# Expert layer on one core: the gates of the first dense tile placed by 128 indirect transfers with addition

## The chip, the core and the metric

One NeuronCore of one Trainium2 chip runs one program. Its engines work side by side and meet only at semaphores: TensorE (PE in the profile, with its weight loads as PEld), VectorE (DVE), ScalarE (ACT), GpSimd (POOL) and the sync engine (SP), which issues most of the DMA transfers. The metric is the device time of one execution in microseconds. Three runs of the kernel before took 1687.2, 1688.26 and 1694.93 us, median 1688.26.

## The reference

One layer of a decoder on 512 tokens of width 1024, all in f32. A conditioning vector gives shift, scale and gate for two sub-layers. Sub-layer 1 mixes tokens (a gated unit and an attention with forgetting). Sub-layer 2, around which this change lies, retrieves single-neuron experts: each token has 8 heads, each head picks 16 of 16384 experts by products of two sub-keys, so that a token has 128 picks. Cut to what matters:

```
q = (xt @ w_query).reshape(t, 8, 2, 128)
scores = einsum('thpd,hpnd->thpn', q, sub_keys)
sv, si = top_k(scores, 16)                       # 16 rows i and 16 columns j of a 128 x 128 grid
cand   = sums of the 16 x 16 pairs;  top_s, pos = top_k(cand, 16)
idx    = i * 128 + j at pos;         gate = softmax(top_s)      # 8 heads x 16 picks per token
out[t] = sum over picks e of  gate[t,e] * gelu(expert_u[idx[t,e]] . x[t]) * expert_v[idx[t,e]]
```

Two heads of a token may pick the same expert, one head never picks one twice. After it come the gated residual and a final RMSNorm.

## The kernel before

The 512 tokens are four tiles of 128. Tile 0 is the sparse one: for each of its 128 picks GpSimd gathers 128 rows of `expert_u` (4 KB each, one per token) by an indirect transfer, and VectorE takes the dot product with the token (`dot`, L1497); later the same is done with `expert_v` (`add`, L1503). The gathered rows go through a ring of 8 places, four in `shared` and four in `hT`.

Tiles 1 to 3 are the dense ones. Their activations are computed for all 16384 experts: `products` (L1097 to L1099) multiplies a block m of 128 experts with the 384 tokens, 24 matmuls of 384 columns, for m = 0 to 127. ScalarE rounds the block (`round_u`, L764), VectorE takes the rest of the rounding (`rest_of_u`, L1490, always one block ahead) and ScalarE reads the result through gelu (L772) and SP stores it. Afterwards `outputs` (L1152 to L1156) multiplies gate times gelu with `expert_v`, again for all experts. For this the gates must stand in a dense array: `g_dram` (`gates_dense`), 24 groups of 16 tokens, each of 128 x (128 x 16) numbers, 1 MB, with the expert's j as row, then i and token.

The dense gates of a tile are built by one-hot products. When its picks and gates are known (`gates`, L1464, signal `gates_ready`), PE transposes i, j and gate (`turn`, L921) and ScalarE copies them (L814). Then for each half group of 8 tokens VectorE writes two one-hot arrays by comparison with a ramp (`hot_rows`, L1477), ScalarE scales one of them by the gates (`gate_rows`, L784), PE multiplies them per token (`build`, L1112: 8 matmuls) and ScalarE copies the two banks (`copy_built`, L793). Per 16 tokens SP stores a group.

The order of all this is written out by hand, alike on each engine. In the loop over n = 1, 2, 3 the selection of tile n runs on VectorE in 11 segments, between which `BESIDE[n]` products stand (3 in all for n = 1, 18 for n = 2 and for n = 3); then `gates(n)`, one product (`BEFORE_TURN`), the turn, two products (`AFTER_TURN`), and 16 steps of one half group's build and one product each. These last are called the chunks of the tile here. In the chunks VectorE takes 4 and 3 dots in turn per group of 16 tokens, so 28 per tile. So n = 1 holds products 0 to 21, n = 2 holds 22 to 58, n = 3 holds 59 to 95. The products 96 to 111 stand in a loop with two dots each (`LOOP_AT` = 12, counted in bodies of 8), and the last 16 with 12 dots.

GpSimd issues the gathers in program order (`gather_rows`, L589 and L601): rows 0 to 3 as soon as tile 0's picks are known, rows 4 to 7 after the turn of the first dense tile, each later row when the dot that used its place is done. A dot waits for the gather of its row; VectorE works in program order, so whatever stands behind the dot waits too, and `rest_of_u` stands there, for which the next product on PE waits.

Of the kernel before, what the change touches and what calls it, by code (L numbers as in the profile page):

```python
# [67 lines left out]
LOOP_AT = 12  # L68
DOTS_BESIDE = (4, 3)
DOTS_IN_CHUNKS = DENSE * CHUNKS // 2 * sum(DOTS_BESIDE)  # L70
# [34 lines left out]
def plan_banks():  # L105
# [28 lines left out]
    jobs += [(("turn", d), 5) for d in range(DENSE)]  # L134
# [7 lines left out]
def program(nc, x, cT, w_ada, b_ada, norm1_g, w_in, b_f, sg_ln_g, sg_ln_b, sg_wT, sg_bT,  # L142
# [5 lines left out]
    with ExitStack() as ctx:  # L148
# [107 lines left out]
        g_dram = nc.dram_tensor("gates_dense", (GROUPS, P, NKEYS * GROUP), F32).ap()  # L256
        a_dram = nc.dram_tensor("gelu_dense", (NKEYS // A_STEPS, P, A_STEPS * DTOK), F32).ap()
# [14 lines left out]
        turned = ada[:, 2 * D:2 * D + 6 * P].rearrange("p (b c t) -> p b c t", b=2, c=3)  # L272
        iota128 = ada[:, 2 * D + 6 * P:2 * D + 7 * P]
# [59 lines left out]
        gates_ready, iota_made = sem("gates_ready"), sem("iota_made")  # L333
        hot_made, hot_gated, built = sem("hot_made"), sem("hot_gated"), sem("built")
# [49 lines left out]
        def _(sp):  # L384
# [53 lines left out]
            sp.dma_start(keysT, sub_keysT).then_inc(keys_in, 16)  # L438

# [17 lines left out]
            for n in range(1, NT):  # L457
# [69 lines left out]
        def _(pool):  # L527
# [11 lines left out]
            link(nc.gpsimd.memset(gate[:, :], 1.0))  # L539
            link(nc.gpsimd.memset(tri, 1.0))  # L540
# [42 lines left out]
            def gather_rows(table, which, used):  # L583

                def one_round(i, half, first):
# [17 lines left out]

                one_round(0, 0, True)
                one_round(0, 1, False)
# [10 lines left out]
        def _(act):  # L617
# [161 lines left out]
            def gate_rows(half):  # L779
                act.wait_ge(hot_made, half + 1)  # L780
                for q in range(HTOK):
                    token = half % (P // HTOK) * HTOK + q
                    rows = hot_i[:, half % HALVES, q, :]
                    ins = nc.scalar.activation(rows, rows, ACT.Copy, scale=turned[:, half * HTOK // P % 2, 2, token:token + 1])  # L784
# [15 lines left out]
            for n in range(1, NT):  # L800
# [860 lines left out]
```

## Time and profile before

| | us |
|---|---|
| median of the runs | 1688.26 |
| the profiled execution | 1689.51 |
| its span, first to last instruction | 1687.8 |
| PE busy | 1587.2 (94%) |
| DVE busy | 1258.3 (75%) |
| ACT busy | 664.9 (39%) |
| POOL busy | 391.9 (23%) |
| mean granted TensorE clock | 0.98 |

The profile is of one execution. All durations are read from it, and the profiled execution's own time is 1.7 us above its span. Up to some 490 us the first sub-layer and the queries run, from some 495 to 1132 us the 128 products with the three builds beside them, then the outputs. A busy PE is not a PE at its peak, since matmuls overlap; the pace of a stage is read from the distance of equal instructions instead.

### The profile page before, as it was taken

The numbers are of one execution on the slowest core, as the hardware profiler recorded it, in microseconds if no ns is written. First come the engines' busy times: TensorE is split into PE (matmuls) and PEld (weight loads), VectorE is DVE, ScalarE is ACT, GpSimd is POOL, SyncE is SP. The second block draws the span as 40 slices with busy tenths as digits, with TensorE's granted clock in tenths as the row PEclk, the third lists the DMA queues.
The fourth block names the chain that finished last, engine by engine and source line by source line (L and its number), as shares of the span: only waits on it lengthen the run. The fifth ranks groups of instructions, "written<-read, shape, count | busy, mean of one in ns | idle before, by whom it ended". The sixth has DMA issues, their size and how long they took to land.

```text
span 1687.8 us, 22615 instructions
## 1 busy us (share of the span) xinstructions
PE 1587.2 (94%) x7605; PEld 1292.7 (77%) x7605; DVE 1258.3 (75%) x2268; ACT 664.9 (39%) x1227; POOL 391.9 (23%) x326
## 2 busy tenths in 40 slices
PE   1899988999999999999989999799999999999995
PEld 0454465554559999999989999798888888888884
DVE  6448364439957987899788988558888878788887
ACT  2111132221337852588336853233333333333333
POOL 1101400000002320033001346413344334334420
PEclk9989989999999999999999999999999999999998
DMA  9765420000127994489736999987999999999982
GB/s 361 275 229 181 149 76 0 1 0 1 50 85 278 363 360 150 160 325 357 278 135 224 361 387 413 402 314 261 367 352 345 354 357 354 329 362 359 344 315 87
DMA packets 172770, 426.26 MB, mean 253 GB/s; under 512 B 13068, under 2 KB 62220, under 8 KB 169496
## 3 DMA queue, kind: packets, MB, share of 16 engines
q1 hardware_dynamic: 86400, 265.89, 42.2%
q0 software_dynamic: 36864, 134.23, 21.8%
q10 hardware_dynamic: 49432, 25.19, 5.3%
q8 instruction: 41, 0.67, 0.2%
q14 instruction: 33, 0.27, 0.0%
HBM read 372.84 MB, written 52.43 MB: 252 GB/s over the span
## 4 chain that ended last, share of the span: by engine, by line
PE 87%; DVE 6%; DMA 3%; ACT 2%; issue 1%; ACTq 1%; SPq 0%; DVEq 0%
PE bank L1152 10%; PE bank L1153 10%; PE bank L1156 10%; PE bank L1097 10%; PE bank L1099 10%; PE bank L1098 10%; PE bank L1043 7%; PE bank L951 5%; PE bank L1112 5%; PE bank L1026 3%; PE bank L961 3%; PE bank L921 1%; DMA weights<-in_w_ada 1%; PE bank L1053 1%; ACTq L842 1%
## 5 line engine op out<-in xcount | busy, mean ns | idle before, releaser
L1097 PE MATMUL bank<-h_hi,u_hi 128*128 128x384 f32 x1024 | 350.7, 343 | 22.0 <-DVE u_lo L1490 13.2
L1098 PE MATMUL bank<-h_lo,u_hi 128*128 128x384 f32 x1024 | 345.0, 337 | 0.0
L1099 PE MATMUL bank<-h_hi,u_lo 128*128 128x384 f32 x1024 | 345.0, 337 | 0.0
L1152 PE MATMUL bank<-v_hi,w_hi 128*128 128x512 f32 x768 | 299.2, 390 | 1.7 <-DVE w_lo L1597 1.6
L1153 PE MATMUL bank<-v_lo,w_hi 128*128 128x512 f32 x768 | 298.8, 389 | 0.0
L865 ACT ACTIVATE v_hi<-weights 128x1024 fp32r<-128x1024 f32 x128 | 135.8, 1061 | 330.2 <-PE bank L1156 264.3
L1156 PE MATMUL bank<-v_hi,w_lo 128*128 128x512 f32 x768 | 236.4, 389 | 0.0
L1593 DVE TENSOR_TENSOR v_lo<-weights,v_hi 128x1024 fp32r<-128x1024 f32 x128 | 157.7, 1232 | 95.2 <-ACT v_hi L865 93.0
L1490 DVE TENSOR_TENSOR u_lo<-weights,u_hi 128x1024 fp32r<-128x1024 f32 x128 | 155.9, 1223 | 95.8 <-PE bank L1099 72.7
L1097 PEld LDWEIGHTS bank<-h_hi,u_hi 128*128 128x128 f32 x1024 | 194.7, 190 | 25.3 <-DVE u_lo L1490 12.8
L1098 PEld LDWEIGHTS bank<-h_lo,u_hi 128*128 128x128 f32 x1024 | 194.8, 190 | 0.0
L1099 PEld LDWEIGHTS bank<-h_hi,u_lo 128*128 128x128 f32 x1024 | 194.3, 190 | 0.0
L1152 PEld LDWEIGHTS bank<-v_hi,w_hi 128*128 128x128 f32 x768 | 144.1, 188 | 33.4 <-DVE v_lo L1593 2.4
L1156 PEld LDWEIGHTS bank<-v_hi,w_lo 128*128 128x128 f32 x768 | 144.2, 188 | 30.0
L1153 PEld LDWEIGHTS bank<-v_lo,w_hi 128*128 128x128 f32 x768 | 144.2, 188 | 29.7
L601 POOL DMA_INDIRECT hT<-in_expert_u,idx_slot x64 | 78.6, 1228 | 290.1 <-DVE hT L1497 200.7
L601 POOL DMA_INDIRECT hT<-in_expert_v,idx_slot x64 | 102.8, 1606 | 172.6 <-DVE y L1503 157.3
L1477 DVE TENSOR_TENSOR weights<-ada 128x1024 f32<-128x1024 f32 x96 | 113.5, 1224 | 35.8 <-PE bank L1112 24.2
L764 ACT ACTIVATE u_hi<-weights 128x1024 fp32r<-128x1024 f32 x128 | 135.1, 1057 | 0.8 <-DMA weights<-in_uT 0.8
L784 ACT ACTIVATE weights<-weights,ada 128x128 f32<-128x128 f32 x384 | 117.7, 389 | 38.5 <-DVE weights L1477 38.5
L601 POOL DMA_INDIRECT shared<-in_expert_v,idx_slot x64 | 90.4, 1412 | 179.1 <-DVE y L1503 149.3
L601 POOL DMA_INDIRECT shared<-in_expert_u,idx_slot x64 | 72.6, 1134 | 204.4 <-DVE shared L1497 187.3
(233 smaller groups left out, 2179.6 us busy)
## 6 DMA issues: line engine op xcount, KB each, us to landing
weights<-in_uT SPq DMA_DIRECT2D x128, 512.0 KB
weights<-in_expert_v SPq DMA_DIRECT2D x128, 512.0 KB, 7.8
weights<-in_w_ada SPq DMA_DIRECT2D x12, 2048.0 KB, 10.3
gates_dense<-weights SPq DMA_DIRECT2D x24, 1024.0 KB
weights<-gates_dense ACTq DMA_DIRECT2D x16, 1536.0 KB
shared<-gelu_dense SPq DMA_DIRECT2D x64, 384.0 KB, 8.9
gelu_dense<-weights SPq DMA_DIRECT2D x32, 384.0 KB
gelu_dense<-ada SPq DMA_DIRECT2D x32, 384.0 KB
```

The lines of the kernel that those rows point to most:

```text
L601: nc.gpsimd.indirect_dma_start(ring(r % ROWS), None, table, bass.IndirectOffsetOnAxis(idx_slot[:, half, r:r + 1], 0))\
L764: nc.scalar.activation(u_hi[:, r % RAW, :], u_raw[:, r % RAW, :], ACT.Copy).then_inc(u_hi_made, 1)
L865: nc.scalar.activation(v_hi[:, r % 2, :], v_raw[:, r % RAW, :], ACT.Copy).then_inc(v_hi_made, 1)
L1043: ins = nc.tensor.matmul(b[:, :], h2T(t)[:, k, :], w[:, k, :], start=(k == 0), stop=(k == KC - 1))
L1097: nc.tensor.matmul(a, uh[:, k, :], h2_hi[:, :, k, :], start=(k == 0), stop=False)
L1098: nc.tensor.matmul(a, uh[:, k, :], h2_lo[:, :, k, :], start=False, stop=False)
L1099: ins = nc.tensor.matmul(a, ul[:, k, :], h2_hi[:, :, k, :], start=False, stop=(k == KC - 1))
L1152: nc.tensor.matmul(acc, wh, v_hi[:, r % 2, cols], start=begin, stop=False)
L1153: nc.tensor.matmul(acc, wh, v_lo[:, r % RAW, cols], start=False, stop=False)
L1156: ins = nc.tensor.matmul(acc, wl, v_hi[:, r % 2, cols], start=False, stop=end)
L1490: tt(u_lo[:, r % LOW, :], u_raw[:, r % RAW, :], u_hi[:, r % RAW, :].bitcast(F32), ALU.subtract).then_inc(u_lo_made, 1)
L1593: tt(v_lo[:, r % RAW, :], v_raw[:, r % RAW, :], v_hi[:, r % 2, :].bitcast(F32), ALU.subtract).then_inc(v_lo_made, 1)
```

## The change

The first dense tile (`d` = 0, n = 1) is no longer built by one-hot products. Its part of `g_dram`, 8 groups, is filled with zeros by 8 transfers of SP from `gate_sparse`, which GpSimd has set to zero at the start; they stand behind the load of the sub-keys, and `gates(0)` waits for them before it writes `gate_sparse`. `gates(1)` writes the normalised gates and, in two more small instructions, the address of each pick in `g_dram` (`sent_gate`, `sent_place`); a constant per token (`token_place`) is made in five small instructions on VectorE beforehand. GpSimd then issues 128 indirect transfers, one for each pick (head h, place k): each sends 128 single f32 numbers, one per token, from SBUF to `g_dram`, and adds them to what stands there. The 16 transfers of a head follow one another freely, since their addresses are all different; ahead of the first of the next head GpSimd waits until all before have landed, since two heads of a token may have the same address. In GpSimd's order they stand between the first round of gathers (rows 0 to 7) and the second (rows 8 to 15).

The transposes, the one-hot arrays, the scaling, the build matmuls, the copies and the stores of this tile go, and with them the 16 steps of its chunks: n = 1 holds products 0 to 5, n = 2 holds 6 to 42, n = 3 holds 43 to 79, and the loop takes products 80 to 111 (`LOOP_AT` = 10). The 28 dots that stood in the first tile's chunks move: dots 0 to 27 now stand in the chunks of n = 2, 28 to 55 in those of n = 3, and 64 instead of 32 in the loop. ScalarE waits for all transfers ahead of its first load of gates. The rest is index arithmetic. Its core:

```diff
+SCATTERED = 1
+BUILT = DENSE - SCATTERED
+LOOP_AT = 10
 DOTS_BESIDE = (4, 3)
-DOTS_IN_CHUNKS = DENSE * CHUNKS // 2 * sum(DOTS_BESIDE)
+DOTS_IN_CHUNKS = BUILT * CHUNKS // 2 * sum(DOTS_BESIDE)
...
+        g_places = g_dram.rearrange("g p n -> (g p n)").rearrange("(n a) -> n a", a=1)
...
+        sent_gate, sent_place = [[turned[:, d % 2, c] for d in range(SCATTERED)] for c in range(2)]
+        sent_place = [p.bitcast(U32) for p in sent_place]
+        token_place = misc[:, 96:97]
+        token_low, token_u = misc[:, 97:98], misc[:, 98:99].bitcast(U32)
...
+            sp.wait_ge(zeros_made, 1)
+            for g in range(SCATTERED * CHUNKS):
+                sp.dma_start(g_dram[g].rearrange("p (a n) -> p a n", n=NSEL),
+                             gate_sparse[:, :].unsqueeze(1).broadcast_to([P, NKEYS * GROUP // NSEL, NSEL])).then_inc(g_zeroed, 16)
...
-                for c in range(CHUNKS):
+                for c in range(CHUNKS if n > SCATTERED else 0):
                     for h in range(HALVES):
                         product(m, m % BODY)
                         m += 1
-                    g = (n - 1) * CHUNKS + c
+                    g = (n - 1 - SCATTERED) * CHUNKS + c
                     sp.wait_ge(build_read, (g + 1) * GROUP // BATCH)
-                    sp.dma_start(g_dram[g], staging[g % 2].rearrange("p i t -> p (i t)")).then_inc(g_stored[g % 2], 16)
+                    sp.dma_start(g_dram[SCATTERED * CHUNKS + g], staging[g % 2].rearrange("p i t -> p (i t)")).then_inc(g_stored[g % 2], 16)
...
+            nc.gpsimd.memset(gate_sparse[:, :], 0.0).then_inc(zeros_made, 1)
+            nc.gpsimd.iota(token_u, [[1, 1]], base=0, channel_multiplier=1).then_inc(token_made, 1)
...
                             if r == ROWS // 2 and not which:
-                                wait_full(pool, "turn", 0)
+                                pool.wait_ge(places_ready, 1)
...
+                def scatter(d, h):
+
+
+                    if h == 0:
+                        pool.wait_ge(places_ready, d + 1)
+                    if d == 0 and h == 0:
+                        pool.wait_ge(g_zeroed, 16 * SCATTERED * CHUNKS)
+                    else:
+                        pool.wait_ge(scattered, 16 * TOPK * (d * PH + h))
+                    for k in range(h * TOPK, (h + 1) * TOPK):
+                        nc.gpsimd.indirect_dma_start(g_places, bass.IndirectOffsetOnAxis(sent_place[d][:, k:k + 1], 0),
+                                                     sent_gate[d][:, k:k + 1], None, compute_op=ALU.add).then_inc(scattered, 16)
+
                 one_round(0, 0, True)
+                for d in range(0 if which else SCATTERED):
+                    for h in range(PH):
+                        scatter(d, h)
                 one_round(0, 1, False)
...
-                for _ in range(BEFORE_TURN):
+                for _ in range(BEFORE_TURN if d >= SCATTERED else BEFORE_TURN + AFTER_TURN):
                     product(m)
                     m += 1
+                if d < SCATTERED:
+                    continue
+                e = d - SCATTERED
                 b = wait_full(act, "turn", d)
-                if d >= 2:
-                    act.wait_ge(hot_gated, (d - 1) * P // HTOK)
+                if d >= 2 and d - 2 < SCATTERED:
+                    act.wait_ge(scattered, 16 * NSEL * (d - 1))
+                elif d >= 2:
+                    act.wait_ge(hot_gated, (e - 1) * P // HTOK)
                 release(nc.scalar.activation(turned[:, d % 2], b[:, 0:3 * P].rearrange("p (c t) -> p c t", c=3), ACT.Copy), "turn", d)
                 product(m)
                 m += 1
-                gate_rows(d * P // HTOK)
+                gate_rows(e * P // HTOK)
                 product(m)
                 m += 1
-                gate_rows(d * P // HTOK + 1)
-                for h in range(HALVES * d * CHUNKS, HALVES * (d + 1) * CHUNKS):
+                gate_rows(e * P // HTOK + 1)
...
-                act.wait_ge(g_stored[b], 16 * GROUPS // 2)
-            act.wait_ge(built, DTOK // BATCH)
+                act.wait_ge(g_stored[b], 16 * BUILT * CHUNKS // 2)
+            act.wait_ge(scattered, 16 * NSEL * SCATTERED)
+            act.wait_ge(built, BUILT * P // BATCH)
...
+                if d < SCATTERED:
+                    for _ in range(AFTER_TURN):
+                        product(m)
+                        m += 1
+                    continue
+                e = d - SCATTERED
+                pe.wait_ge(gates_ready, e + 1)
                 transposes(("turn", d), [picks(n)[2], picks(n)[3], gate[:, :]])
...
-                if n >= 2:
+                if n - 2 >= SCATTERED:
...
-                into = (gate if n else gate_sparse)[:, :].rearrange("p (h k) -> p h k", h=PH)
+                if n == 0:
+                    dve.wait_ge(g_zeroed, 16 * SCATTERED * CHUNKS)
+                into = gate_sparse[:, :] if n == 0 else sent_gate[n - 1] if n <= SCATTERED else gate[:, :]
+                into = into.rearrange("p (h k) -> p h k", h=PH)
                 ins = tt(into, gh, gate_sum.unsqueeze(2).broadcast_to([P, PH, TOPK]), ALU.mult)
-                if n:
+                if n > SCATTERED:
                     ins.then_inc(gates_ready, 1)
                 else:
                     link(ins)
+                if 0 < n <= SCATTERED:
+
+                    sel_i, sel_j = picks(n)[2:4]
+                    link(stt(out=sel_j, in0=sel_j, scalar=float(NKEYS), in1=sel_i, op0=ALU.mult, op1=ALU.add))
+                    ts(sent_place[n - 1], sel_j, float(GROUP), token_place, ALU.mult, ALU.add).then_inc(places_ready, 1)
+                    if n > 1:
+                        dve.wait_ge(places_ready, n)
...
+            dve.wait_ge(token_made, 1)
+            link(nc.vector.tensor_copy(token_place, token_u))
+            link(ts(token_u, token_u, GROUP - 1, None, ALU.bitwise_and))
+            link(nc.vector.tensor_copy(token_low, token_u))
+            link(tt(token_place, token_place, token_low, ALU.subtract))
+            link(stt(out=token_place, in0=token_place, scalar=float(P * NKEYS), in1=token_low, op0=ALU.mult, op1=ALU.add))
```

On GpSimd (POOL), at the first round of gathers, this stands in a row before (L601 are the gathers, `bank5_full` is the turn of the first dense tile):

```order
L601 DMA shared<-in_expert_u,idx_slot 128x1024 [waits idx_staged]
L601 DMA shared<-in_expert_u,idx_slot 128x1024 x3
L601 DMA hT<-in_expert_u,idx_slot 128x1024 [waits bank5_full]
L601 DMA hT<-in_expert_u,idx_slot 128x1024 x3
L589 COPY idx_slot<-idx 128x8
L601 DMA shared<-in_expert_u,idx_slot 128x1024 [waits idx_staged,dot_done]
L601 DMA shared<-in_expert_u,idx_slot 128x1024 [waits dot_done] x3
```

And now (L617 are the gathers, L631 the transfers with addition), first the beginning of the piece and then its end:

```order
L617 DMA shared<-in_expert_u,idx_slot 128x1024 [waits idx_staged]
L617 DMA shared<-in_expert_u,idx_slot 128x1024 x3
L617 DMA hT<-in_expert_u,idx_slot 128x1024 [waits places_ready]
L617 DMA hT<-in_expert_u,idx_slot 128x1024 x3
L631 DMA gates_dense<-ada 6291456x1 [waits g_zeroed,places_ready]
L631 DMA gates_dense<-ada 6291456x1 x15
L631 DMA gates_dense<-ada 6291456x1 [waits scattered]
L631 DMA gates_dense<-ada 6291456x1 x15
```

```order
L631 DMA gates_dense<-ada 6291456x1 x15
L631 DMA gates_dense<-ada 6291456x1 [waits scattered]
L631 DMA gates_dense<-ada 6291456x1 x15
L605 COPY idx_slot<-idx 128x8
L617 DMA shared<-in_expert_u,idx_slot 128x1024 [waits idx_staged,dot_done]
L617 DMA shared<-in_expert_u,idx_slot 128x1024 [waits dot_done] x3
```

Between the gather of row 7 and that of row 8 there are now 128 transfers and eight waits; nothing else of GpSimd's program has moved.

On VectorE, at the gates of the first dense tile (L1461 to L1464), before, with the first one-hot arrays (L1477) and dots (L1497) behind them:

```order
L1490 TENSOR_TENSOR u_lo<-weights,u_hi 128x1024 x4
L1461 TENSOR_REDUCE misc<-gate 128x8
L1462 RECIPROCAL misc<-misc 128x8
L1464 TENSOR_TENSOR gate<-gate,misc 128x128
L1490 TENSOR_TENSOR u_lo<-weights,u_hi 128x1024
L1477 TENSOR_TENSOR weights<-ada 128x1024 x2
L1490 TENSOR_TENSOR u_lo<-weights,u_hi 128x1024
L1477 TENSOR_TENSOR weights<-ada 128x1024 x2
L1490 TENSOR_TENSOR u_lo<-weights,u_hi 128x1024
L1477 TENSOR_TENSOR weights<-ada 128x1024 x2
L1490 TENSOR_TENSOR u_lo<-weights,u_hi 128x1024
L1497 SCALAR_TENSOR_TENSOR shared,act_w<-shared,y 128x1024 x2
```

And now, with the address's two instructions (L1520, L1521) and the selection of the next tile (L1410 and on) right behind:

```order
L1545 TENSOR_TENSOR u_lo<-weights,u_hi 128x1024 x4
L1506 TENSOR_REDUCE misc<-gate 128x8
L1507 RECIPROCAL misc<-misc 128x8
L1512 TENSOR_TENSOR ada<-gate,misc 128x128
L1520 SCALAR_TENSOR_TENSOR hT<-hT 128x128
L1521 TENSOR_SCALAR ada<-hT,misc 128x128
L1545 TENSOR_TENSOR u_lo<-weights,u_hi 128x1024 x3
L1410 MAX final_row<-shared 128x8 x8
L1413 MAX_INDEX final_row<-final_row,shared 128x8 x8
```

The 16 steps with one-hot arrays are gone from this place, and with them the first 28 dots.

On VectorE, in the chunks of the second dense tile, before; these dots are numbers 28 and on:

```order
L1477 TENSOR_TENSOR weights<-ada 128x1024 x2
L1490 TENSOR_TENSOR u_lo<-weights,u_hi 128x1024
L1477 TENSOR_TENSOR weights<-ada 128x1024 x2
L1490 TENSOR_TENSOR u_lo<-weights,u_hi 128x1024
L1497 SCALAR_TENSOR_TENSOR hT,act_w<-hT,y 128x1024 x2
L1477 TENSOR_TENSOR weights<-ada 128x1024 x2
L1490 TENSOR_TENSOR u_lo<-weights,u_hi 128x1024
L1497 SCALAR_TENSOR_TENSOR hT,act_w<-hT,y 128x1024 x2
L1477 TENSOR_TENSOR weights<-ada 128x1024 x2
```

And now at the same place, dots 0, 1, 2 and on (L1552):

```order
L1532 TENSOR_TENSOR weights<-ada 128x1024 x2
L1545 TENSOR_TENSOR u_lo<-weights,u_hi 128x1024
L1552 SCALAR_TENSOR_TENSOR shared,act_w<-shared,y 128x1024 x2
L1532 TENSOR_TENSOR weights<-ada 128x1024 x2
L1545 TENSOR_TENSOR u_lo<-weights,u_hi 128x1024
L1552 SCALAR_TENSOR_TENSOR shared,act_w<-shared,y 128x1024 x2
L1532 TENSOR_TENSOR weights<-ada 128x1024 x2
L1545 TENSOR_TENSOR u_lo<-weights,u_hi 128x1024
L1552 SCALAR_TENSOR_TENSOR hT,act_w<-hT,y 128x1024
L1532 TENSOR_TENSOR weights<-ada 128x1024 x2
L1545 TENSOR_TENSOR u_lo<-weights,u_hi 128x1024
L1552 SCALAR_TENSOR_TENSOR hT,act_w<-hT,y 128x1024 x2
```

The dots that stand in the second tile's chunks are now the first ones of all, and the ninth of them needs a row that GpSimd gathers only behind the 128 transfers.

## Rows read from the trace of the kernel before

**Rows 1.** The page: busy time by engine; the chain by engine and line.

```profile
PE 1587.2 (94%) x7605; PEld 1292.7 (77%) x7605; DVE 1258.3 (75%) x2268; ACT 664.9 (39%) x1227; POOL 391.9 (23%) x326
...
PE 87%; DVE 6%; DMA 3%; ACT 2%; issue 1%; ACTq 1%; SPq 0%; DVEq 0%
PE bank L1152 10%; PE bank L1153 10%; PE bank L1156 10%; PE bank L1097 10%; PE bank L1099 10%; PE bank L1098 10%; PE bank L1043 7%; PE bank L951 5%; PE bank L1112 5%; PE bank L1026 3%; PE bank L961 3%; PE bank L921 1%; DMA weights<-in_w_ada 1%; PE bank L1053 1%; ACTq L842 1%
```

**Rows 2.** ACT timeline, gelu reads (L772): start us, us, what, [idle before <-releaser].

```profile
511.01 0.49 ACT L772 ACTIVATE ada<-bank 128x384 f32<-128x384 f32 x1 [2.72 <-PE bank L1099]
...
619.19 0.49 ACT L772 ACTIVATE weights<-bank 128x384 f32<-128x384 f32 x1 [2.62 <-issue]
...
623.35 0.49 ACT L772 ACTIVATE ada<-bank 128x384 f32<-128x384 f32 x1 [2.72 <-PE bank L1099]
```

**Rows 3.** The chain in order of time, 490 to 720: start us, us, what.

```profile
524.00 1.78 PE bank L1112 x16
```

**Rows 4.** Busy us (instructions) by engine, then PEclk, DMA share, GB/s, by window.

```profile
525.42:614.62 89.20, 89.20 (x603) 89.20 (x602) 81.23 (x97) 70.83 (x173) 29.71 (x29) 1.00 0.97 355
623.35:706.51 83.16, 78.08 (x439) 76.97 (x438) 68.40 (x230) 29.21 (x40) 0.00 (x0) 0.98 0.51 172
1004.77:1050.45 45.68, 45.68 (x266) 45.68 (x265) 38.58 (x55) 15.87 (x22) 29.49 (x25) 1.00 1.03 414
```

**Rows 5.** DVE timeline around the gates of the first dense tile.

```profile
490.84 1.23 DVE L1484 TENSOR_TENSOR h_lo<-y,h_hi 128x1024 fp32r<-128x1024 f32 x1 [6.06 <-PE bank L1043]
...
508.61 0.29 DVE L1464 TENSOR_TENSOR gate<-gate,misc 128x128 f32<-128x128 f32 x1
```

**Rows 6.** POOL timeline: indirect transfers, each with its idle time before.

```profile
433.12 0.95 POOL L601 DMA_INDIRECT shared<-in_expert_u,idx_slot  x1 [0.30 <-issue]
434.37 0.95 POOL L601 DMA_INDIRECT shared<-in_expert_u,idx_slot  x1 [0.30 <-issue]
...
518.37 1.96 POOL L601 DMA_INDIRECT hT<-in_expert_u,idx_slot  x1 [0.30 <-issue]
520.64 1.97 POOL L601 DMA_INDIRECT hT<-in_expert_u,idx_slot  x1 [0.30 <-issue]
...
531.27 1.17 POOL L601 DMA_INDIRECT shared<-in_expert_u,idx_slot  x1 [7.21 <-DVE shared L1497]
532.75 1.07 POOL L601 DMA_INDIRECT shared<-in_expert_u,idx_slot  x1 [0.30 <-issue]
...
557.80 1.05 POOL L601 DMA_INDIRECT shared<-in_expert_u,idx_slot  x1 [0.89 <-POOL idx_slot L589]
```

**Rows 7.** DVE timeline, first and ninth dot in the second dense tile's chunks.

```profile
719.88 1.22 DVE L1497 SCALAR_TENSOR_TENSOR hT<-hT,y 128x1024 f32<-128x1024 f32 x1
...
744.81 1.22 DVE L1497 SCALAR_TENSOR_TENSOR hT<-hT,y 128x1024 f32<-128x1024 f32 x1
```

**Rows 8.** DMA queues and issues: KB each, us to landing.

```profile
q0 software_dynamic: 36864, 134.23, 21.8%
...
out<-xs SPq DMA_DIRECT2D x4, 512.0 KB, 2.7
...
ada<-in_norm_g SPq DMA_DIRECT2D x1, 512.0 KB, 3.7
...
misc<-in_cT SPq DMA_DIRECT2D x1, 4.0 KB, 1.7
```

**Rows 9.** SP timeline after the last loads, and a window of the attention.

```profile
218.69 0.34 SPq L438 DMA_DIRECT2D ada<-in_sub_keysT  x1
...
255.00:375.00 120.00, 108.85 (x443) 62.68 (x442) 48.15 (x93) 32.63 (x64) 0.00 (x0) 1.00 0.00 1
```

**Rows 10.** The chain from 1060 to 1110, and ACT behind it.

```profile
1068.49 12.32 DMA weights<-in_uT
...
1081.89 14.01 ACTq L842
...
1103.09 0.49 ACT L772 ACTIVATE weights<-bank 128x384 f32<-128x384 f32 x1 [4.38 <-PE bank L1099]
```

More of the change, by code:

```diff
@@ L133, in plan_banks @@
         jobs += query_jobs(n, QUERY_PAIRS[0]) + query_jobs(n, QUERY_PAIRS[1])
-    jobs += [(("turn", d), 5) for d in range(DENSE)]
+    jobs += [(("turn", d), 5) for d in range(SCATTERED, DENSE)]
     place, count = {}, [0] * 8
@@ L333, in program @@
         gates_ready, iota_made = sem("gates_ready"), sem("iota_made")
+        zeros_made, g_zeroed, token_made = sem("zeros_made"), sem("g_zeroed"), sem("token_made")
+        places_ready, scattered = sem("places_ready"), sem("scattered")
         hot_made, hot_gated, built = sem("hot_made"), sem("hot_gated"), sem("built")
@@ L783, in gate_rows @@
                     rows = hot_i[:, half % HALVES, q, :]
-                    ins = nc.scalar.activation(rows, rows, ACT.Copy, scale=turned[:, half * HTOK // P % 2, 2, token:token + 1])
+                    ins = nc.scalar.activation(rows, rows, ACT.Copy,
+                                               scale=turned[:, (SCATTERED + half * HTOK // P) % 2, 2, token:token + 1])
                 ins.then_inc(hot_gated, 1)
@@ L816, in _ @@
                 m += 1
-                gate_rows(d * P // HTOK)
+                gate_rows(e * P // HTOK)
                 product(m)
                 m += 1
-                gate_rows(d * P // HTOK + 1)
-                for h in range(HALVES * d * CHUNKS, HALVES * (d + 1) * CHUNKS):
+                gate_rows(e * P // HTOK + 1)
+                for h in range(HALVES * e * CHUNKS, HALVES * (e + 1) * CHUNKS):
                     copy_built(2 * h)
@@ L826, in _ @@
                     m += 1
-                    if h + HALVES < HALVES * (d + 1) * CHUNKS:
+                    if h + HALVES < HALVES * (e + 1) * CHUNKS:
                         gate_rows(h + HALVES)
@@ L1129, in _ @@
                     m += 1
-                if d == 0:
+                if e == 0:
                     for t in range(NT):
@@ L1133, in _ @@
                             wait_read(pe, "h2T", t, s)
-                for h in range(HALVES * d * CHUNKS, HALVES * (d + 1) * CHUNKS):
+                for h in range(HALVES * e * CHUNKS, HALVES * (e + 1) * CHUNKS):
                     build(h)
@@ L1159, in _ @@
             wait_read(pe, "turn", DENSE - 1)
-            pe.wait_ge(build_read, DTOK // BATCH)
+            pe.wait_ge(build_read, BUILT * P // BATCH)
             for r in range(BODY):
@@ L1475, in hot_rows @@
                 for which, rows in ((1, hot_j), (0, hot_i)):
-                    key = turned[:, half * HTOK // P % 2, which, at:at + HTOK]
+                    key = turned[:, (SCATTERED + half * HTOK // P) % 2, which, at:at + HTOK]
                     ins = tt(rows[:, half % HALVES], iota128.unsqueeze(1).broadcast_to([P, HTOK, P]),
@@ L1526, in _ @@
                 gates(n)
-                for _ in range(BEFORE_TURN):
+                for _ in range(BEFORE_TURN if d >= SCATTERED else BEFORE_TURN + AFTER_TURN):
                     product(m)
                     m += 1
+                if d < SCATTERED:
+                    continue
+                e = d - SCATTERED
                 wait_read(dve, "turn", d)
                 for h in range(HALVES):
-                    hot_rows(d * P // HTOK + h)
+                    hot_rows(e * P // HTOK + h)
                     product(m)
                     m += 1
-                for h in range(HALVES * d * CHUNKS, HALVES * (d + 1) * CHUNKS):
-                    if h + HALVES < HALVES * (d + 1) * CHUNKS:
+                for h in range(HALVES * e * CHUNKS, HALVES * (e + 1) * CHUNKS):
+                    if h + HALVES < HALVES * (e + 1) * CHUNKS:
                         hot_rows(h + HALVES)
```

2 lines of the change are left out of this document (removed).

## The prediction

> **What bounds the kernel now.** I read the page first. PE is busy for 94% of the span and makes 87% of the chain that ended last, with the build matmuls (L1112) as 5% of it [rows 1]. A busy PE may still be paced by another engine, so the second view is ScalarE's timeline, cut down to the gelu that reads each product: its distances are the pace. Without builds it is 4.16 us (619.19 to 623.35), with them 5.95 (15 steps in the 89.20 us of the first window) [rows 2, 4]. The chain says why: in each chunk step the 16 records of one build take 1.78 us of the path [rows 3], and 4.16 + 1.78 is 5.94. PE sets the pace in both, with VectorE at 91% of the window beside it (81.23 of 89.20 us) [rows 4]. What the change takes off PE is therefore worth its full length there.
>
> The other thing to see is how VectorE, PE and GpSimd hang together. VectorE runs in program order, PE needs its `u_lo` for each product and gets it one product ahead. A dot stands between two of them and waits for a row that GpSimd gathered. In the kernel before GpSimd is far ahead: it has nothing at all to do from 623 to 706 us [rows 4]. The change fills just this time, and the question is whether it ends in time.
>
> **What goes.** From the gelu of product 2 (511.01) to that of product 22 (623.35) are 20 products in 112.34 us [rows 2]. At 4.16 each they take 83.2, so the turn and the 16 builds of the first dense tile cost 29.1 us beyond the products, 28.5 of them 16 times 1.78 [rows 3]. The 16 products themselves move to the loop, where 11 of them take 45.68 us with two dots each, 4.15 apiece [rows 4]. Gain: **-29.1 us**. The stores, copies and scalings of this tile lie beside PE's work and give nothing more.
>
> **What is hidden.** GpSimd's memset and ramp at the start stand before all work. The five small instructions for `token_place` stand ahead of the second selection, at whose end VectorE waits 6.06 us for PE [rows 5]; they are far shorter than that, so 0, and at most some 2 us without this cover. The zeros are 8 MB behind the sub-keys, issued at 218.69; in a window of 120 us behind them the DMA share is 0.00 [rows 9], and SP's next work comes at some 490 us. At a quarter of the 355 GB/s of [rows 4] 8.4 MB take 94 us and still end inside that window. 0.
>
> **The 128 transfers.** The places are ready two small instructions behind the gates at 508.61, so at 509.5 [rows 5]. First come the gathers of rows 4 to 7. From start to start one costs 1.25 us (433.12 to 434.37, VectorE in selection work), 1.48 (531.27 to 532.75, beside dots and `u_lo`) or 2.27 (518.37 to 520.64, where one-hot arrays are written) [rows 6]. Four at 1.48 end at 515.4.
>
> A scatter of single numbers with addition isn't in the trace. Each addresses 128 rows as a gather does, and GpSimd makes the descriptors for as many, so gathers are the nearest rows. Lower end 0.95, the duration of one without the 0.30 gap (here no other signal stands between two transfers); upper end 2.27. VectorE does selection work most of this time, with a `u_lo` every 4.16 us, so I take 1.30, near the first kind: 128 x 1.30 = 166.4. On top come seven waits between heads, each from the last issue to its landing. Small transfers land in 1.7 (4 KB in), 2.7 (a 512 KB store to HBM) or 3.7 us (a 512 KB load by row) [rows 8]; I take the store's 2.7, so 18.9. T = 185.3, from 133.5 (128 x 0.95 + 7 x 1.7) to 316.5 (128 x 2.27 + 7 x 3.7). GpSimd is through at 700.7.
>
> The page "DMA: Bandwidth & Descriptors" of the Trainium skill (Anatomy of one DMA) puts the fixed cost of such a transfer at about 2.0 us, nearly all of it the receipt of the write. By it the seven waits would be 14 and not 18.9 us, and the forecast 5 us lower; the landing times of 1.7 to 3.7 here agree with it.
>
> Behind the transfers GpSimd copies the next indices and waits for the copy (0.89 us ahead of the start at 557.80 [rows 6], 1.0 with the copy), issues the gather of row 8 (1.3) and it lands (3.7): 706.7.
>
> **When row 8 is wanted.** The first eight dots have their rows. The ninth stands 24.9 us behind the first of its tile's chunks (719.88, 744.81) [rows 7]. That is 121.5 us behind the gelu at 623.35, with which the segments of n = 2 begin. In the changed kernel that gelu comes 29.1 + 16 x 4.16 = 95.7 us earlier, so the ninth dot is due at 649.1. VectorE is one product ahead, which covers 4.2 us. The stall is S = 706.7 - 649.1 - 4.2 = **+53.4 us**. Behind GpSimd's transfers wait the gathers of rows 8 to 15, behind the dot on VectorE wait the one-hot arrays and `u_lo`, behind these PE. Nothing gives it back later: the stages behind are at PE's pace. In general S = T - 132.
>
> Two small terms. After the stop near 1090 us the next gelu waits 4.38 us where 2.72 is usual [rows 2, 10], so +1.6 for the restart. And the loop with two gathers per product gets 16 products longer. It moves 414 GB/s with a DMA share of 1.03 [rows 4], right at its limit; what a product asks for (three times 0.524 MB and 0.197 MB of stores) in 4.16 us is 425. Over 16 products the missing 11 GB/s are 0.7 MB, 1.8 us, which lengthens the wait that stands there already (12.32 us for `u`, 14.01 for ScalarE's issue of the gate load [rows 10]). I take +2, from 0 to 10 (the whole ring of 8 rows late, 4.2 MB at 414).
>
> **Sum.** -29.1 + 53.4 + 1.6 + 2.0 = +27.9. Against the profiled execution, 1689.5, that is 1717.4. The median of the runs lies 1.2 below that execution, so **1716 us**.
>
> **Rivals.** *The transfers are cheap.* GpSimd might need less for a single number than for a row, and without the gap. At the lower end T is 133.5 and S 1.6, the sum -24 and the time 1664; below T = 132 the gain is whole and the time 1661. For it speaks the missing signal between two transfers; against it that no start to start in the trace is below 1.25 us, which already gives T = 179. It decides at T = 157.5, 1.08 us per transfer, where the sum is zero.
>
> *In between.* 1.02 to 1.15 us per transfer leave the time within 0.5%: the stall eats the gain and no more.
>
> *GpSimd is disturbed.* A gather takes 1.96 us instead of 0.95 where VectorE writes one-hot arrays [rows 6], two inputs from SBUF at once. If the same happened beside all of the transfers, T is 316.5, S 184.5 and the time 1847. Against it: in this stretch VectorE mostly selects, and beside that the duration was 0.95.
>
> The page "SBUF - State Buffer" of the Trainium skill (Who interferes with whom) says that a `tensor_tensor` with both inputs in SBUF contends with GpSimd's reads only, and infers that making descriptors needs the write side. By this no transfer is disturbed, each costs 1.25 and the time is 1710. The 1.96 us of the row speak against it, so I don't go by it.
>
> *The DMA engines are the pace.* The gathers' queue took 21.8% of 16 engines' span for 36864 packets [rows 8], 0.16 us each, 9 per engine and transfer. If adding one number takes an engine as long as moving one such packet, a transfer takes 1.44 us, T is 203 and the time 1734. If it takes twice that, since the old value must be read first, T is 387, S 255 and the time 1918. A full round trip of 1.7 us for each number, one after the other, would be 15 us per transfer and nearly 2 ms; that end is there, but in the trace packets of one queue overlap.
>
> **How the numbers follow.** A change of 0.5%, 8.4 us, is about what can be told from none here. Forecast with its neighbours (1.15 to 1.75 us per transfer, GpSimd or DMA as the pace): 0.50. Cheap transfers: 0.18. In between: 0.12. Disturbed or paced at 1.75 us and more: 0.20. Faster therefore 0.18, same 0.12, slower 0.70. The range goes from the cheap end, 1663, to 1800, which is a T of 270; it leaves some 0.05 below and 0.13 above. The likeliest case alone has 1698 to 1775.
>
> **What would show it.** In the profile after: 128 transfers on GpSimd from some 515 to 700 us, their start to start near 1.3 and seven gaps of some 2.7; a stop of VectorE before its ninth dot, near 650 us, of some 55 us with the gather as what ended it; products at 4.16 us from product 0 on to product 26, without the step to 5.95 near 525; a third of the build line's records gone; the loop's pace still 4.16. If the last transfer is over before 650, the forecast is wrong and the gain stands. If the starts are right and the stop is absent, my reading of the dots' order is wrong. If the products before 625 us are slower than 4.16, the transfers disturb something that I have left out.

## The result and the profile after

The changed kernel takes 1806.6 us, median of 4 runs (1804.6 to 1807.7), where the kernel before takes 1689.5 beside it. The ratio is 1.069, with a 95% interval of 1.067 to 1.071: slower by 117 us. The span of the profiled execution went from 1687.8 to 1802.9, so +115.1.

The page of the changed kernel: busy time, the chain by engine and line, and the group of the 128 transfers (L631; busy, mean ns | idle before).

```profile
PE 1560.3 (87%) x7346; PEld 1266.4 (70%) x7346; DVE 1224.4 (68%) x2243; ACT 609.3 (34%) x1066; POOL 633.3 (35%) x456
...
q0 software_dynamic: 55296, 134.31, 22.9%
...
PE 73%; POOL 12%; DVE 5%; DMA 4%; issue 4%; ACT 2%; ACTq 1%; SPq 0%; DVEq 0%; POOLq 0%
POOL gates_dense L631 11%; PE bank L1197 9%; PE bank L1198 9%; PE bank L1201 9%; PE bank L1136 7%; PE bank L1137 7%; PE bank L1138 7%; PE bank L1082 6%; PE bank L990 5%; PE bank L1065 3%; PE bank L1000 3%; PE bank L1151 2%; DMA gates_dense<-ada 1%; PE bank L960 1%; DMA weights<-in_w_ada 1%
...
L631 POOL DMA_INDIRECT gates_dense<-ada x128 | 217.3, 1698 | 55.5 <-issue 41.6
```

GpSimd now stands on the chain with 12%, where it did not stand at all [rows 1]. A transfer takes it 1698 ns on average, and the queue of its transfers has 55296 packets instead of 36864 [rows 8], 144 more for each of the 128.

GpSimd's timeline where the transfers begin, where VectorE has stopped, and at their end (columns as in [rows 6]):

```profile
514.94 0.94 POOL L617 DMA_INDIRECT hT<-in_expert_u,idx_slot  x1 [0.30 <-issue]
516.18 2.05 POOL L631 DMA_INDIRECT gates_dense<-ada  x1 [0.31 <-issue]
...
547.18 1.56 POOL L631 DMA_INDIRECT gates_dense<-ada  x1 [0.30 <-issue]
551.25 1.56 POOL L631 DMA_INDIRECT gates_dense<-ada  x1 [2.50 <-DMA gates_dense<-ada]
...
559.65 3.21 POOL L631 DMA_INDIRECT gates_dense<-ada  x1 [0.30 <-issue]
...
663.99 1.56 POOL L631 DMA_INDIRECT gates_dense<-ada  x1 [0.30 <-issue]
665.86 1.56 POOL L631 DMA_INDIRECT gates_dense<-ada  x1 [0.30 <-issue]
...
787.17 1.56 POOL L631 DMA_INDIRECT gates_dense<-ada  x1 [0.30 <-issue]
...
789.83 1.02 POOL L617 DMA_INDIRECT shared<-in_expert_u,idx_slot  x1 [0.90 <-POOL idx_slot L605]
```

The transfers run from 516.2 to 788.7 us, so T, the prediction's name for the length of this block, is 272.6. At rest one takes 1.56 us and the next starts 0.30 later (663.99 to 665.86). Beside VectorE's work, up to 653 us, 16 of the first 60 take 2.0 to 3.2 us (559.65). Between two heads GpSimd idles 2.50 us and less (551.25).

VectorE around its ninth dot (L1552), and ScalarE's reads of the products around it, the first of them to be held beside [rows 2]:

```profile
648.67 1.22 DVE L1552 SCALAR_TENSOR_TENSOR hT<-hT,y 128x1024 f32<-128x1024 f32 x1
...
794.42 1.23 DVE L1552 SCALAR_TENSOR_TENSOR shared<-shared,y 128x1024 f32<-128x1024 f32 x1 [144.53 <-DMA shared<-in_expert_u,idx_slot]
```

```profile
511.29 0.49 ACT L804 ACTIVATE ada<-bank 128x384 f32<-128x384 f32 x1 [2.72 <-PE bank L1138]
...
527.93 0.49 ACT L804 ACTIVATE ada<-bank 128x384 f32<-128x384 f32 x1 [2.72 <-PE bank L1138]
...
650.80 0.48 ACT L804 ACTIVATE ada<-bank 128x384 f32<-128x384 f32 x1
...
800.79 0.47 ACT L804 ACTIVATE weights<-bank 128x384 f32<-128x384 f32 x1
...
806.50 0.47 ACT L804 ACTIVATE weights<-bank 128x384 f32<-128x384 f32 x1
```

The ninth dot, free to go at 649.9, waits 144.53 us for the gather of row 8, and ScalarE sees the next product at 800.79 instead of some 6 us behind 650.80. From 511.29 to 527.93 four products came at 4.16 each: the step to 5.95 that stood there in the kernel before is gone.

The windows of the stop and of the loop (columns as in [rows 4]):

```profile
660.00:785.00 125.00, 0.00 (x0) 0.00 (x0) 0.00 (x0) 0.00 (x0) 97.19 (x63) 0.51 0.20 0
1057.00:1182.00 125.00, 125.00 (x723) 125.00 (x722) 104.84 (x149) 43.27 (x60) 82.92 (x67) 1.00 1.03 413
```

In 125 us nothing works but GpSimd. The DMA engines are busy for 0.20 of it at 0 GB/s, TensorE's granted clock is 0.51, its lower level of 1.2 GHz. Behind the stop TensorE's first product starts at that level. Below are the window of its first 9 records and, for comparison, one from the kernel of the third experiment behind its own shorter stop, with 18:

```profile
799.12:801.85 2.73, 2.73 (x9) 2.73 (x9) 2.73 (x5) 2.73 (x9) 2.43 (x2) 0.50 0.86 297
```

```profile
723.27:728.88 5.61, 5.61 (x18) 5.61 (x19) 5.61 (x8) 4.64 (x13) 4.40 (x4) 0.50 0.96 322
```

Here the next gelu, at 806.50, still comes after 5.71 us, no later than usual with a build, so in this kernel the lower clock costs nothing that shows. In the three kernels below that keep a stop (half of the transfers, without addition, half of the rows) 17 or 18 records ran at the lower level and the same interval is 6.84, 6.87 and 6.77 us instead of 5.89: there it costs about 1 us. The loop runs at its old pace with a DMA share of 1.03, over twice the length.

The balance of the spans: -29.1 for the builds, +144.0 for the stop (149.99 from one gelu to the next instead of 6.01) and +1.5 in the wait ahead of the last products, which is 17.9 us instead of 16.4. That is +116.4 against +115.1 measured.

### The profile page after: what moved, and what is told of

Same layout as the page of the kernel before. It is cut to its first block, busy times and chain, and to the rows that moved or that the text cites. A ratio compares the mean times of both kernels' runs of the same rounds, so it can differ in the third digit from the quotient of the medians.

```text
span 1802.9 us, 22177 instructions
## 1 busy us (share of the span) xinstructions
PE 1560.3 (87%) x7346; PEld 1266.4 (70%) x7346; DVE 1224.4 (68%) x2243; ACT 609.3 (34%) x1066; POOL 633.3 (35%) x456
## 3 DMA queue, kind: packets, MB, share of 16 engines
q0 software_dynamic: 55296, 134.31, 22.9%
## 4 chain that ended last, share of the span: by engine, by line
PE 73%; POOL 12%; DVE 5%; DMA 4%; issue 4%; ACT 2%; ACTq 1%; SPq 0%; DVEq 0%; POOLq 0%
POOL gates_dense L631 11%; PE bank L1197 9%; PE bank L1198 9%; PE bank L1201 9%; PE bank L1136 7%; PE bank L1137 7%; PE bank L1138 7%; PE bank L1082 6%; PE bank L990 5%; PE bank L1065 3%; PE bank L1000 3%; PE bank L1151 2%; DMA gates_dense<-ada 1%; PE bank L960 1%; DMA weights<-in_w_ada 1%
## 5 line engine op out<-in xcount | busy, mean ns | idle before, releaser
L631 POOL DMA_INDIRECT gates_dense<-ada x128 | 217.3, 1698 | 55.5 <-issue 41.6
L1552 DVE SCALAR_TENSOR_TENSOR shared<-shared,y 128x1024 f32<-128x1024 f32 x64 | 76.5, 1220 | 146.4 <-DMA shared<-in_expert_u,idx_slot 146.3
L617 POOL DMA_INDIRECT hT<-in_expert_v,idx_slot x64 | 113.2, 1769 | 171.0 <-DVE y L1558 141.0
L617 POOL DMA_INDIRECT hT<-in_expert_u,idx_slot x64 | 83.6, 1306 | 241.4 <-DVE hT L1552 156.7
L617 POOL DMA_INDIRECT shared<-in_expert_v,idx_slot x64 | 94.7, 1480 | 178.9 <-DVE y L1558 164.3
L816 ACT ACTIVATE weights<-weights,ada 128x128 f32<-128x128 f32 x256 | 78.5, 389 | 170.1 <-DVE weights L1532 170.1
```

The costliest lines, as they stand in the source:

```text
L617: nc.gpsimd.indirect_dma_start(ring(r % ROWS), None, table, bass.IndirectOffsetOnAxis(idx_slot[:, half, r:r + 1], 0))\
L631: nc.gpsimd.indirect_dma_start(g_places, bass.IndirectOffsetOnAxis(sent_place[d][:, k:k + 1], 0), sent_gate[d][:, k:k + 1], None, compute_ ...
```

## The experiments

The first four ran on one chip, where the kernel before took 1687.6 us.

**No transfer.** In `gather_rows` and at ScalarE's last wait (its wait for the transfers ahead of a later turn goes as well):

```diff
-                    for h in range(PH):
-                        scatter(d, h)
+                    pass
...
-            act.wait_ge(scattered, 16 * NSEL * SCATTERED)
```

> Leaves out all 128 transfers (the gates of the first dense tile stay zero); zeros, addresses and the order of everything else stay. Theory A (the loss is the row that stands behind the transfers on GpSimd, and nothing else): VectorE's wait of 144.5 us before the ninth dot is gone, the products come every 4.16 us up to product 21, and the time is 1806.6 - 144.5 + 0 to 4 for what was covered, so 1662 to 1666; that is the -29 us of the builds and +2 for the longer loop against 1689.5. Rival B (a part of the loss is in the zeros, the addresses or the longer loop): above 1672.

1661.1 us (1659.7 to 1662.8), ratio 0.983 (0.980 to 0.986). A second time, on another chip, 1660.4 and 0.985 (0.983 to 0.987). Theory A holds, and the time is even a little below its 1662 to 1666. Of the 29.1 us that the builds are worth 26.5 and 26.7 arrive, so zeros, addresses and the longer loop cost together some 2.5 us, and the whole loss comes with the transfers. The difference of the profiled spans is 1802.9 - 1661.0 = 141.9 (144.7 against the second one's 1658.2), and the products alone differ by 144, against a wait of 144.5.

**Half of the transfers** (ScalarE's waits count half as many).

```diff
-                    for h in range(PH):
+                    for h in range(PH // 2):
```

> Leaves out the last four of the eight heads, so 64 transfers remain. Theory A: they end where the first 64 of the changed kernel end, at 660.4 us, row 8 lands some 5.7 us later, at 666, and the ninth dot, due at 649.9, waits some 16 us; PE loses some 12 of them and the time is about 1674 to 1680. A stall in proportion to the number of transfers (half of 144.5) would give 1734, so the point T = 132 from which the transfers cost anything is tested too. Rival B (disturbance by additions all over the stage): half of the loss, about 1734.

```profile
L631 POOL DMA_INDIRECT gates_dense<-ada x64: 1559/1564/2590, 516.1 to 656.6; - x64
```

```profile
DVE shared L1552 <- DMA shared<-in_expert_u,idx_slot: 12.6, 1, 12.6
```

(A source view: duration in ns min/median/max, first and last start. A waits view: us in total, times, longest.) 1679.4 us, ratio 0.994 (0.991 to 0.996). Half of the transfers do not cost half of 144.5: VectorE waits 12.6 us. The loss has a threshold. Before the ninth dot is due some 130 us of transfers are free, behind it each costs its full length. T minus VectorE's wait is 129.5 here (656.6 + 1.6 - 516.1 = 142.1), and 128.1 with all of them.

**Transfers without addition.**

```diff
-                                                     sent_gate[d][:, k:k + 1], None, compute_op=ALU.add).then_inc(scattered, 16)
+                                                     sent_gate[d][:, k:k + 1], None).then_inc(scattered, 16)
```

> The 128 transfers write their numbers without adding (where two heads of a token pick the same expert the later one stays, so the sum of such pairs is left out). Tells what makes one transfer 1.56 us on GpSimd where a gather of a row takes 0.94. If it is the addition (the old value has to be described too), one falls to about 0.95, T to about 128 x 1.25 + 128 x 0.25 of disturbance + 14 = 206 and the time to about 1740. If it is the single number or the direction into HBM, 1.56 stays and the time is 1800 to 1810.

```profile
L631 POOL DMA_INDIRECT gates_dense<-ada x128: 963/967/1982, 515.9 to 711.9; - x128
```

```profile
DVE shared L1552 <- DMA shared<-in_expert_u,idx_slot: 69.0, 1, 69.0
```

```profile
q0 software_dynamic: 40960, 134.31, 21.0%
```

1730.7 us, ratio 1.024 (1.021 to 1.027). The transfer falls from 1563 to 967 ns, as long as a gather at rest [rows 6], T falls to 711.9 + 1.0 - 515.9 = 197 and the wait to 69.0. So it is the addition that costs GpSimd 0.60 us, not the single number and not the direction; what GpSimd does in that time is not shown. The packets change too: 40960 - 36864 are 32 per plain transfer, and with addition it is 144. But they are not what GpSimd's time follows: a gather also has 144 (36864 for 256 of them [rows 8]) and takes 0.95 [rows 6].

**Half of the rows in each transfer.** On another chip, one run:

```diff
-bass.IndirectOffsetOnAxis(sent_place[d][:, k:k + 1], 0), sent_gate[d][:, k:k + 1], ...
+bass.IndirectOffsetOnAxis(sent_place[d][0:P // 2, k:k + 1], 0), sent_gate[d][0:P // 2, k:k + 1], ...
```

> Each of the 128 transfers sends only the numbers of tokens 0 to 63 (the other half of the first dense tile's gates is left out). Tells whether a transfer costs GpSimd by its rows or by itself. By rows: 0.78 us instead of 1.56, T about 173 and the time about 1705. By itself: 1.56 and 1806. A plain transfer took 0.97 and one with addition 1.56; if these are a fixed part and one per row with two descriptors against three, it lies between, near 0.9, T near 190 and the time near 1720.

```profile
L631 POOL DMA_INDIRECT gates_dense<-ada x128: 1405/1410/3510, 517.0 to 767.1; - x128
```

```profile
q0 software_dynamic: 47104, 134.28, 22.0%
```

1789.6 us, with T at 251.5 and VectorE's wait at 125.0. My middle guess is wrong: 64 rows take 1410 ns and 128 take 1563, by these two points an estimated 2.4 ns per row and 1.26 us for the transfer itself. Smaller transfers hardly help GpSimd; whether fewer and fuller ones would wasn't run. A transfer has 80 packets now ((47104 - 36864) / 128), so with addition it is one per number and 16 more.

**The transfers spread over GpSimd's program.** The addition stays, the whole layer is computed. Gates and addresses get a stretch of `ada` of their own, so that the third tile's turn needn't wait for the transfers, and behind the gather of each row some transfers follow (the first rounds of gathers are written out for it instead of looped):

```diff
-        sent_gate, sent_place = [[turned[:, d % 2, c] for d in range(SCATTERED)] for c in range(2)]
+        sent_gate, sent_place = [ada[:, 2 * D + 7 * P:3 * D]], [ada[:, 3 * D:3 * D + P]]
...
+def sent_after(row):
+    # transfers behind the gather of a row: 128 in all
+    return {7: 48, 35: 35}.get(row, 1 if row > 7 and row % 5 else 0)
...
+                        if not which and isinstance(i, int):
+                            for _ in range(sent_after((2 * i + half) * STAGED + r)):
+                                next(transfers)
```

> All 128 transfers, but spread over GpSimd's program: 48 (three heads) behind the gather of row 7, 35 behind that of row 35, the others one at a time behind the gathers of rows 8 to 63, in four of five. The gates and places lie in a stretch of their own, so that no turn waits for the transfers. Theory A: 48 transfers end near 624 us, before row 8's place is free, no dot waits long, and the time is that of the kernel without transfers, 1662 to 1668, 1.4% under the kernel before. Rival B (it is the work of the transfers, wherever they stand): GpSimd's and the DMA's extra work slows the chunks, and the time is above 1680.

1675.9 us, ratio 0.993 (0.990 to 0.996). The stop is gone and the kernel is faster than before, but 15 us above the kernel without transfers, between the two theories. Up to product 80 its products keep, but for fractions, that kernel's distances; then 82, 84 and 86 take 8.4, 8.8 and 6.9 us. VectorE waits there for gathers (waits from 905 to 950 us):

```profile
DVE shared L1562 <- DMA shared<-in_expert_u,idx_slot: 9.7, 5, 4.2
...
DVE hT L1562 <- DMA hT<-in_expert_u,idx_slot: 6.1, 3, 4.2
```

**Another division:** `{7: 54, 35: 44}`, 10 beside rows 8 to 27, 20 beside rows 36 to 55.

> As e4_spread with another division: 54 transfers behind row 7, 10 beside rows 8 to 27, 44 behind row 35, 20 beside rows 36 to 55. e4_spread lost its 12 us where the loop begins (products 82 to 86 at up to 8.8 us), with transfers until 923 us. Theory A (GpSimd runs late there because its transfers stand in the last chunks, where it has no time left beside the gathers; the transfers cost nothing where GpSimd would wait anyway): this stop is gone, the time is 1661 to 1666, the same as without any transfer, and 1.3 to 1.6% under the kernel before. Rival B (the transfers cost the stage something wherever they stand, some 0.1 us each): it stays near 1675.

1672.4 us, ratio 0.990 (0.988 to 0.992), between the two theories. The products keep the pace of the kernel without transfers up to 76, and again lose it where the last transfers stand in the chunks (waits from 895 to 925 us):

```profile
DVE hT L1562 <- DMA hT<-in_expert_u,idx_slot: 10.9, 4, 5.6
```

**A third division:** `{7: 54, 35: 46}`, one behind each of rows 8 to 27 and 36 to 43.

> As e5_spread2 with the 128 transfers divided 54 behind row 7, one behind each of rows 8 to 27, 46 behind row 35, one behind each of rows 36 to 43. In e5_spread2 the products kept the pace of the kernel without transfers up to product 76 and lost 1 us at 77 to 79, 5 us at 81 and 2.5 us in the loop, where the DMA share is 1.03 and a late ring is not made up. Theory A (what costs is a ring of gathered rows that is not full when the loop begins; transfers that end well before it are free): within 0.2% of the kernel without transfers on the same chip, about 1661 to 1665, 1.5% under the kernel before. Rival B (the transfers cost the stage wherever they stand): it stays 8 us or more above the kernel without them.

> The kernel of e1_none once more (all 128 transfers left out), on the chip of e7_spread3, so that the two can be compared: 1661, the bound of what any order of the transfers can reach.

1686.6 us, ratio 1.000 (0.998 to 1.001), 26 us above the 1660.4 of the kernel without transfers. The expectation failed, and GpSimd's timeline (L639 transfers, L622 gathers) says why:

```profile
646.73 1.66 POOL L622 DMA_INDIRECT shared<-in_expert_u,idx_slot  x1 [0.30 <-issue]
648.69 2.53 POOL L639 DMA_INDIRECT gates_dense<-ada  x1 [0.30 <-issue]
651.52 1.67 POOL L622 DMA_INDIRECT shared<-in_expert_u,idx_slot  x1 [0.30 <-issue]
653.49 2.54 POOL L639 DMA_INDIRECT gates_dense<-ada  x1 [0.30 <-issue]
656.34 1.40 POOL L622 DMA_INDIRECT hT<-in_expert_u,idx_slot  x1 [0.30 <-issue]
```

Beside one-hot work a gather and a transfer take 4.8 us together from 646.73 to 651.52, and 28 dots in 95 us want a row every 3.4. One transfer per gather doesn't fit, one for two gathers (4.8 + 1.7 = 6.5 us, where two dots last 6.8) just does. GpSimd also waited 6.1 us in this stretch for transfers to land between two heads, which can have added to its lateness. The second division, with one transfer for two gathers beside the same rows, lost nothing there. VectorE waits again (675 to 760 us):

```profile
DVE shared L1562 <- DMA shared<-in_expert_u,idx_slot: 18.6, 4, 7.4
...
DVE hT L1562 <- DMA hT<-in_expert_u,idx_slot: 6.6, 2, 5.6
```

**A fourth division, by that budget:** `{7: 56, 35: 46}`, 10 beside rows 8 to 27, 12 beside rows 36 to 59, 4 in the loop.

> The 128 transfers divided by what GpSimd has left: 56 behind row 7, 10 beside rows 8 to 27 (as e5_spread2, which lost nothing there; e7_spread3 with 20 lost some 40 us of pace from product 36 on), 46 behind row 35, 12 beside rows 36 to 59 (e5_spread2 had 20 in 20 rows and lost 8.5 us), 4 in the loop. Theory (GpSimd's time is a budget: a gather and a transfer beside one-hot work take some 4.5 us together where a dot comes every 3.4 us, so one transfer for two gathers fits and one for each doesn't): 1661 to 1666, within 0.3% of the kernel without transfers (1660.4). Rival (the budget is full everywhere, so each transfer moved is only paid elsewhere): 1670 or more, as e4_spread and e5_spread2.

```profile
DVE hT L1562 <- DMA hT<-in_expert_u,idx_slot: 1.6, 1, 1.6
DVE shared L1562 <- DMA shared<-in_expert_u,idx_slot: 1.0, 1, 1.0
```

1666.6 us, ratio 0.990 (0.986 to 0.993). Five of the six runs lie from 1662.9 to 1668.2; the sixth took 1683.8, at a mean granted clock of 0.93 where they have 0.98. (The 40 us that the expectation names for the third division were misjudged; it was 26.) The waits at the loop's begin are down to 2.6 us, and its profiled span of 1664.6 lies 3.6 and 6.4 above those of the two kernels without transfers (1661.0 and 1658.2); the median lies 5.5 and 6.2 above theirs, 0.6 above the expected range and well below the rival's 1670. The chunks keep their pace to within 1 us, as the budget says; the rest is lost in small steps, 2.3 us of it in the loop, and their cause stays open. By the ratio it can't be told from the second division, which ran on another chip. These two are the best that I found, 1.0% under the kernel before, of the 1.5 to 1.7% that the kernel gains without any transfer.

## Why the prediction was wrong

It named the mechanism and the side, with 0.7 for slower, and missed the size: +28 us forecast, +117 measured, and the range ended at 1800.

- **What goes, -29.1.** Right. Without transfers the kernel is 1.5 to 1.7% faster (1661.1 against 1687.6 and 1660.4 against 1687.1), 27 us, which is the 29.1 less what the small terms take, and products 2 to 6 stand 4.16 apart. They don't all do so up to product 26, as the signs had it: product 16 takes 9.44 us in the selection. The kernel before has the same step (9.43) at product 32, so it moves nothing.
- **What is hidden.** Right. SP needed 26.3 us from 216.6 to issue the zeros, and the ninth dot was due at 649.9, 0.8 behind the forecast; two small instructions of 0.29 us each are all that was added ahead of the first places.
- **The place of the stop.** Right: the ninth dot, 649.1 forecast and 649.9 measured, behind row 8's gather.
- **The 128 transfers: the step that failed.** "GpSimd makes the descriptors for as many, so gathers are the nearest rows" priced one at 1.30 us from start to start, without the waits between heads. Measured are 2.02 on average ((272.6 - 14.0) / 128; at rest 1.56 + 0.30, 1.87 from start to start). Of the 87 us that T is longer than the forecast 185.3, the addition makes 128 x 0.60 = 76, as the kernel without it shows. The remaining 11 are there without addition as well (197 against 185.3): there the transfers take 15 us more than forecast, 1.42 instead of 1.30 each, and the waits 3.4 less (15.5 against 18.9). Beside VectorE's work, until 653 us, a quarter of the transfers with addition take 2 us and more, and afterwards, with VectorE still, nearly all take 1.56. A plain transfer costs what a gather does, so the rows of before priced all but the addition, and that had no row. I had written the cost of reading the old value into the rival for the DMA engines and left it out of GpSimd's own price.
- **The waits between heads.** Seven of some 2.0 us, 14.0 in total, where I took 2.7. The 2.0 of the Trainium skill's page "DMA: Bandwidth & Descriptors" (Anatomy of one DMA) was closer than my row of a 512 KB store; counted from the start of an issue, a transfer here lands after 3.1.
- **From T to the time.** S = T - 132 gives 140.6 for T = 272.6, and VectorE waited 144.5. The 4.2 us that a product in reserve was to cover weren't there: 12.6 us of VectorE's wait lengthened the interval of that product from 6.0 to 18.0 us in the kernel with half of the transfers. In the chunks VectorE works 91% of the time [rows 4]; that this leaves it nothing in reserve is my reading, not shown by itself. Together the wait is 91 us longer than the forecast 53.4: 87 by T and 4 by the missing reserve, and that is the miss of 89, but for the small terms.
- **The small terms.** The restart was to cost 1.6; it cost nothing that shows in this kernel and about 1 us in the three others with a stop, so that nothing shows here is a matter of timing and no rule. The longer loop kept its pace at 413 GB/s; the wait behind it grew by 1.5, for which 2 was forecast.
- **The rivals.** GpSimd disturbed throughout (2.27 per transfer, 1847) came nearest in size and for the wrong reason: of the 272.6 us some 17 are disturbance (217.3 us busy against 128 x 1.563). The DMA engines as the pace are refuted, with 0.20 of their time in the stop. What I drew from the Trainium skill's page "SBUF - State Buffer" (Who interferes with whom), that no transfer would be disturbed by a `tensor_tensor`, is not borne out: with one-hot work beside them transfers took 2.53 instead of 1.56 us. The page's rule itself, contention with GpSimd's reads only, may still hold, since a transfer reads its indices from SBUF; that wasn't tested.

The bounds are to blame for the range. The upper end of one transfer, 2.27, lay above the measured 2.02, and T up to 316 stood in the text; I cut the range at a T of 270 because I held a price beyond 1.75 for unlikely. For an operation without a row that was too sure. (The likeliest case's 1698 to 1775 should read 1697 to 1774: the 1.2 us between the profiled execution and the median was left out. It changes nothing.)

## What to carry to other kernels

Work moved to an idle engine is free only up to the moment at which something queued behind it on that engine is needed; find that row first, and compare it with the whole block's length, in the idle engine's own time and beside the neighbours' work. Divide the block by what the engine has left in each stage: here the same 128 transfers cost 144 us in one piece and 6 to 15 in the three better ways of spreading them, and with one behind every gather of the first chunks 26. And an operation with one property that no row of the trace has (here the addition) needs a price of its own, or a range that reaches both ends.

## What the runs showed of the hardware

- An indirect transfer of 128 single f32 numbers with addition into HBM takes GpSimd 1.56 us, without addition 0.97, a gather of 128 rows of 4 KB 0.94. With addition on 64 rows it takes 1.41.
- With addition each number is a packet (144 per transfer, 80 with 64 rows: 16 more than numbers), without it 32 packets do. GpSimd's time doesn't follow them: a gather with 144 packets takes it 0.94. The DMA engines still were busy for only 0.20 of a stretch with nothing else.
- From the last issue of a head to the release of the next some 2.0 us pass (1.7 to 2.5), and a transfer lands 3.1 us behind its issue (median, from 2.9 to 7.9).
- With TensorE idle for 142 us the granted clock fell to 1.2 GHz (0.51). Behind it 9 records ran at the lower level and the interval of 5.71 us was none the longer; behind idle times of 10, 67 and 122.5 us in three other kernels it was 17 or 18 records, and the interval was 6.8 to 6.9 us instead of 5.9.
- A stage at a DMA share of 1.03 keeps its pace of 4.16 us per product for 30 products, but a ring of rows that is late when it begins is not made up there and shows as products of 7 to 9 us.
